# Where the group-norm variance of the previous head pair stands among the levels of the triangular inverse

## The chip, the cores and the metric

The kernel runs on one core of one Trainium2 chip. Its time is the device time of one execution in microseconds (us). Below, PE is TensorE, ACT is ScalarE, DVE is VectorE and POOL is GpSimd.

## The reference, cut to what matters

The reference is a network of three blocks on 1024 tokens of width 1024. The change touches one stage of the second layer, the RWKV-7 time mix, and there its scan over time with what follows it:

```python
def step(S, inp):
    r_t, w_t, k_t, v_t, a_t, b_t = inp
    sa = jnp.einsum('bhvk,bhk->bhv', S, a_t)
    S = S * w_t[:, :, None, :] + sa[..., None] * b_t[:, :, None, :] + v_t[..., None] * k_t[:, :, None, :]
    y = jnp.einsum('bhvk,bhk->bhv', S, r_t)
    return S, y
...
mean = jnp.mean(y, axis=-1, keepdims=True)
var = jnp.mean(jnp.square(y - mean), axis=-1, keepdims=True)
yn = ((y - mean) * lax.rsqrt(var + RW_GN_EPS)).reshape(B, T, D)
yn = yn * ln_w.astype(f32) + ln_b.astype(f32)
```

There are 16 heads of 64 channels. Also of this stage is the norm of each key, `kk / sqrt(sum(kk * kk))`.

## The kernel before, in words

The function `rw_core` computes the scan in chunks of 64 tokens. Two heads stand side by side on the 128 partitions, so the loop over `m` has eight head pairs, m = 0 to 7. For each pair a triangular matrix of each chunk is inverted, first in 2x2 blocks, then by doubling the block size. There are five levels, 0 to 4. At each of the levels 0 to 3, for each of the two heads h:

- TensorE multiplies (`corrections(m, lev, h)`, L2289, 32 matmuls of 64x32 in the profile's count),
- ScalarE copies the product out of PSUM in two instructions (`keep_correction`, L2507 and L2509),
- TensorE multiplies again (`inverses(m, lev, h)`, L2298, 32 matmuls),
- VectorE adds and transposes (`grow`, L2696 and L2698), and the next level's corrections of that head wait for it.

Level 4, the last, has smaller matmuls of 32x32 (`last_corrections`, L2305, and `last_inverses`, L2312). ScalarE copies with L2507 alone between them, and `whole` on VectorE (L2703) ends it. Then `solutions` (L2321), `bonus_sum` (L2215), `outputs` (L2330, L2345) and the next pair's first products follow on TensorE.

The pair before, m-1, is finished inside pair m. Its chunk states are stepped one after the other (L2223, L2225) while level 0 and level 1 run. ScalarE squares the deviations (`squares`, L2499), TensorE sums them over each head (`variance`, L2215 on `rw_end`, four matmuls of 128x512), ScalarE takes the logarithm (`log_variance`, L2491) and later exp(-0.5 x) of it (`inverse_deviation`, L2495), and VectorE scales with that (`group_norm`, L2663).

The pair after, m+1, is prepared inside pair m, too. The squares of its keys are summed by `key_sum` (L2215 on `rw_next`), and ScalarE takes their logarithm (`log_key`, L2483) and exponential (`inverse_key`, L2487). Then come an affine copy (`blend`, L2464) and another exponential (`decay_until`, L2468). Pair 0 has no pair before it, so no variance. Pair 7 has no pair after it, and ScalarE makes copies of rows for the next stage instead (`high`, L2477).

ScalarE holds the tables of one set of functions at a time. Where a logarithm follows an exponential or the other way round, an `ACT_TABLE_LOAD` stands ahead of the instruction.

The order of the work on each engine is the order in which the code is written; there is no scheduler. Engines wait for one another by semaphores, named in the code (`var_done`, `x_ready`, `dt_ready`). Where the variance stands among the levels on TensorE, in `rw_core`:

```python
inverses(m, 1, 1)
if prior:
    variance(m - 1)
for h in (0, 1):
    corrections(m, 2, h)
```

Of the kernel before, what the change touches and what calls it, by code (L numbers as in the profile page):

```python
# [2048 lines left out]
def rw_core(nc, g, block, nxt, small, mk, xh, xl):  # L2049
# [161 lines left out]
    def _(pe):  # L2211
# [16 lines left out]
        def variance(m):  # L2228
            pe.wait_ge(g.dev_ready.sem, g.dev_ready.base + m + 1)
            head_sum(dev, STEP_BANK, g.var_done)  # L2230
# [122 lines left out]
        for m in range(KD):  # L2353
            prior, following = m > 0, m + 1 < KD
            pe.wait_ge(g.hat_go.sem, g.hat_go.base + m + 1)
            if prior:
                pe.wait_ge(g.y1_ready.sem, g.y1_ready.base + m)
            if not prior:
                pe.wait_ge(g.acc_free.sem, first - 1)
            gram(X_BANK, at, bt, g.gram_n)  # L2360
            if not prior:
                pe.wait_ge(g.bonus_ready.sem, g.bonus_ready.base + 1)
                pe.wait_ge(g.acc_free.sem, first)
            pe.wait_ge(g.hat_ready.sem, g.hat_ready.base + m + 1)
            for j in range(NT):
                transposes(m, j)
                if prior and j:
                    step(m - 1, j if j < 4 else j + 1)
                if j == 3:
                    pe.wait_ge(g.prep_ready.sem, g.prep_ready.base + m + 1)  # L2370
                    pe.wait_ge(g.n_ready.sem, g.n_ready.base + m + 1)
                    gram(X_BANK, bt, rt, g.gram_rb)
                    if prior:
                        step(m - 1, 4)
            gram_ar(m)
            if prior:
                step(m - 1, 9)
            pe.wait_ge(g.rb_ready.sem, g.rb_ready.base + m + 1)
            for h in (0, 1):
                corrections(m, 0, h)  # L2380
                if prior:
                    step(m - 1, 10 + h)
            first_solution(m)
            for h in (0, 1):
                inverses(m, 0, h)
                if prior:
                    step(m - 1, 12 + h)
            for h in (0, 1):
                corrections(m, 1, h)
                if prior:  # L2390
                    step(m - 1, 14 + h)
            inverses(m, 1, 0)
            if following:
                pe.wait_ge(g.w_ready.sem, g.w_ready.base + 2 * m + 2)
                key_sum(m + 1)
            inverses(m, 1, 1)
            if prior:
                variance(m - 1)
            for h in (0, 1):
                corrections(m, 2, h)  # L2400
            for h in (0, 1):
                inverses(m, 2, h)
            for h in (0, 1):
                corrections(m, 3, h)
            for h in (0, 1):
                inverses(m, 3, h)
            for h in (0, 1):
                last_corrections(m, h)
            for h in (0, 1):
                last_inverses(m, h)  # L2410
            if prior:
                pe.wait_ge(g.y_ready.sem, g.y_ready.base + m)
            solutions(m)
            if following:
                bonus_sum(m + 1)
            outputs(m, prior, following)
# [27 lines left out]
    def _(act):  # L2444
# [44 lines left out]
        def log_variance(m):  # L2489
            act.wait_ge(g.var_done.sem, g.var_done.base + m + 1)  # L2490
            nc.scalar.activation(deviation_rates, deviation_rates, ACT.Ln, bias=norm_eps).then_inc(g.log_ready.sem, 1)  # L2491
# [20 lines left out]
        for m in range(KD):  # L2512
            prior, following = m > 0, m + 1 < KD
            act.wait_ge(g.gram_n.sem, g.gram_n.base + m + 1)
            nc.scalar.activation(both_of(Nlow), both(X_BANK)[:, :, 0:BLK], ACT.Copy)
            nc.scalar.activation(both_of(Nc), both(X_BANK)[:, :, BLK:CH], ACT.Copy, scale=lower).then_inc(g.n_ready.sem, 1)
            for j in range(NT):
                keep_tokens(m, j)
            keep_correction(m, 0, 0)
            keep_correction(m, 0, 1)  # L2520
            for h, hd in enumerate(heads):
                act.wait_ge(g.w1_done.sem, g.w1_done.base + 2 * m + h + 1)
                nc.scalar.activation(tok[:, :, W_, hd], bank(SUM_BANK + h), ACT.Copy).then_inc(g.w_ready.sem, 1)
            if following:
                key_copy(m + 1)
                decay(m + 1)
            keep_correction(m, 1, 0)
            if following:
                key_square(m + 1)
            else:  # L2530
                high(0)
            keep_correction(m, 1, 1)
            if following:
                growth(m + 1)
            else:
                high(1)
            if prior:
                squares(m - 1)
            if following:
                log_key(m + 1)  # L2540
            else:
                high(2)
            if prior:
                log_variance(m - 1)
            keep_correction(m, 2, 0)
            keep_correction(m, 2, 1)
            if following:
                inverse_key(m + 1)
            else:
                high(3)  # L2550
            keep_correction(m, 3, 0)
            keep_correction(m, 3, 1)
            if following:
                blend(m + 1)
            else:
                high(4)
            keep_correction(m, LAST, 0)
            if following:
                decay_until(m + 1)
            else:  # L2560
                high(5)
            keep_correction(m, LAST, 1)
            if prior:
                inverse_deviation(m - 1)
            for h, b in ((0, X_BANK), (1, D_BANK)):
                act.wait_ge(g.ug_done.sem, g.ug_done.base + 2 * m + h + 1)
                nc.scalar.activation(GU[:, h], g.ps[:, b:b + 2, :].rearrange("p b (j s) -> p (b j) s", j=4), ACT.Copy).then_inc(g.ug_ready.sem, 1)
            if not following:
                high(6)
            act.wait_ge(g.out_y.sem, g.out_y.base + m + 1)  # L2570
            nc.scalar.activation(paired_chunks(y1), pair(X_BANK), ACT.Copy).then_inc(g.y1_ready.sem, 1)
            if prior:
                act.wait_ge(g.normed.sem, g.normed.base + m)
            else:
                act.wait_ge(g.kept[1].sem, g.kept[1].base)
            act.wait_ge(g.out_z.sem, g.out_z.base + m + 1)
            nc.scalar.activation(paired_chunks(dev), pair(SUM_BANK), ACT.Copy).then_inc(g.z_ready.sem, 1)
# [1773 lines left out]
```

## Time and profile before

| What | Value |
| --- | --- |
| Median of 3 runs | 3553.84 us (3550.99 to 3561.1) |
| The profiled execution | 3547.82 us |
| Its span | 3546.0 us |
| TensorE busy | 3405.1 us, 96% of the span |
| ScalarE busy | 1194.9 us, 34% |
| VectorE busy | 1984.6 us, 56% |
| Mean granted TensorE clock | 0.982 of full speed |

The span is what the trace covers; 1.8 us lie around it. The eight pairs take the stretch from about 1590 to 2070 us of it, one pair some 57 us. Busy shares are means over all the stages, so a step of one pair is to be read from a timeline of that pair. The granted clock is 1.00 where TensorE runs at 2.4 GHz and 0.50 where it runs at 1.2 GHz.

### The profile page before, as it was taken

Reading aid. Unit: us, or ns where it says so; the run is one execution under the profiler, and the core shown is the slowest. Engines: PE = TensorE matmul, PEld = TensorE weight load, DVE = VectorE, ACT = ScalarE, POOL = GpSimd, SP = SyncE. Lnnn points to the kernel's source line nnn. Section 1 sums busy time; section 2 is a strip of 40 time slices with the busy share of each in tenths; the row PEclk is TensorE's granted clock in tenths of the full one; section 3 lists DMA queues with packets and bytes.
Section 4 is the critical chain, followed back from the end, with each engine's and each line's share of the span. In section 5 each row is a group of like instructions: output and inputs, shape, how many; then the busy total and the mean of one; then the engine's idle time right before and its main releaser. Section 6 shows DMA issues by size and latency. Waiting matters only on the chain. (4 is left out here: it accounts for less than half of the span.)

```text
span 3546.0 us, 61071 instructions
## 1 busy us (share of the span) xinstructions
PE 3405.1 (96%) x25028; PEld 2748.4 (78%) x25028; DVE 1984.6 (56%) x2398; ACT 1194.9 (34%) x1597; POOL 1590.5 (45%) x1148
## 2 busy tenths in 40 slices
PE   7998999999999999999999999999999999999989
PEld 5886778888888777888787877888888887674767
DVE  6886565556224652226767647555542458868452
ACT  4654233333102362226465524333310231242221
POOL 3442377775333323334344425877633323560352
PEclk9998999999999999999999999999999999999999
DMA  2111122224311142241212211222332113111212
GB/s 103 48 49 38 33 87 79 80 89 152 109 42 56 40 179 95 95 147 39 85 46 86 68 37 48 88 89 78 111 128 88 52 42 119 61 48 42 101 43 76
DMA packets 74063, 274.58 MB, mean 77 GB/s; under 512 B 8208, under 2 KB 8592, under 8 KB 73360
## 3 DMA queue, kind: packets, MB, share of 16 engines
q1 hardware_dynamic: 68112, 250.79, 20.8%
q10 hardware_dynamic: 5760, 20.97, 1.5%
q8 instruction: 153, 2.51, 0.3%
q14 instruction: 38, 0.31, 0.0%
HBM read 207.77 MB, written 63.96 MB: 77 GB/s over the span
## 5 line engine op out<-in xcount | busy, mean ns | idle before, releaser
L117 POOL TENSOR_TENSOR gap<-ones 128x1 f32<-128x1 f32 x150 | 46.0, 307 | 1238.8 <-PE ps L167 774.4
L120 POOL TENSOR_TENSOR wlo<-wraw,whi 128x1024 fp32r<-128x1024 f32 (+3 forms) x150 | 391.6, 2611 | 12.5
L893 DVE TENSOR_TENSOR h<-ps,h 128x1024 f32<-128x1024 f32 (+1 forms) x56 | 68.5, 1223 | 288.9 <-PE ps L416 259.6
L167 PE MATMUL ps<-xh,whi 128*128 128x512 f32 x640 | 203.0, 399 | 21.6 <-ACT rw_stage L1888 5.1
L167 PE MATMUL ps<-xl,whi 128*128 128x512 f32 x640 | 199.2, 393 | 0.0
L167 PE MATMUL ps<-xh,wlo 128*128 128x512 f32 x640 | 198.7, 392 | 0.0
L1007 POOL TENSOR_TENSOR wlo<-wraw,whi 128x512 fp32r<-128x512 f32 x126 | 166.3, 1335 | 52.6 <-ACT whi L1130 52.6
L118 POOL TENSOR_SCALAR whi<-wraw 128x1024 fp32r<-128x1024 f32 (+3 forms) x150 | 178.9, 1192 | 0.0
L384 ACT ACTIVATE sq<-h 128x1024 f32<-128x1024 f32 x32 | 34.0, 1061 | 394.1 <-DVE h L893 304.0
L2200 POOL TENSOR_TENSOR rw_levels<-rw_levels,rw_masks 128x512 f32<-128x512 f32 x64 | 87.2, 1378 | 177.2 <-PE ps L2289 140.8
L167 PEld LDWEIGHTS ps<-xh,whi 128*128 128x128 f32 x640 | 119.7, 190 | 56.6 <-issue 8.9
L1007 POOL TENSOR_TENSOR ffn_wl<-ffn_wsum,ffn_wh 128x512 fp32r<-128x512 f32 x84 | 111.6, 1328 | 110.7 <-ACT ffn_wh L1130 110.6
L167 PEld LDWEIGHTS ps<-xl,whi 128*128 128x128 f32 x640 | 121.3, 190 | 25.9
L167 PEld LDWEIGHTS ps<-xh,wlo 128*128 128x128 f32 x640 | 121.2, 189 | 25.8
L1288 DVE TENSOR_TENSOR sum_of_squares<-ffn_part,sq 128x512 f32<-128x512 f32 x84 | 132.6, 1578 | 9.3
L1130 ACT ACTIVATE whi<-wraw 128x512 fp32r<-128x512 f32 x126 | 79.2, 630 | 168.9 <-POOL wraw L1002 90.3
L1047 PE MATMUL ps<-xh_sums,whi 128*128 128x512 f32 x336 | 130.9, 390 | 2.2 <-ACT ffn_part L1143 2.2
L1047 PE MATMUL ps<-xh_sums,wlo 128*128 128x512 f32 x336 | 130.7, 389 | 0.0
L1047 PE MATMUL ps<-xl_sums,whi 128*128 128x512 f32 x336 | 130.7, 389 | 0.0
L433 DVE TENSOR_TENSOR sum_of_squares<-sum_of_squares,sq 128x1024 f32<-128x1024 f32 x48 | 93.7, 1951 | 56.9 <-ACT sq L384 38.7
L416 PE MATMUL ps<-xh_sums,whi 128*128 128x512 f32 x384 | 118.4, 390 | 0.4 <-POOL wlo L120 0.4
L416 PE MATMUL ps<-xh_sums,wlo 128*128 128x512 f32 x384 | 118.3, 389 | 0.0
(673 smaller groups left out, 9535.0 us busy)
## 6 DMA issues: line engine op xcount, KB each, us to landing
wraw<-w_ffn_in SPq DMA_DIRECT2D x88, 512.0 KB, 3.5
ffn_hidden<-sum_of_squares SPq DMA_DIRECT2D x44, 512.0 KB, 2.6
rw_next<-rw_kept SPq DMA_DIRECT2D x40, 512.0 KB, 5.1
wraw<-w_ffn_out SPq DMA_DIRECT2D x32, 512.0 KB, 3.6
ffn_stage<-ffn_hidden SPq DMA_DIRECT2D x30, 512.0 KB, 4.9
rw_kept<-rw_stage SPq DMA_DIRECT2D x24, 512.0 KB, 2.7
rw_kept<-rw_stage ACTq DMA_DIRECT2D x24, 512.0 KB, 2.7
wraw<-w_ple SPq DMA_DIRECT2D x16, 640.0 KB, 3.8
```

The costliest lines, as they stand in the source:

```text
L117: nc.gpsimd.tensor_tensor(g.gap[:, 0:1], g.ones[:, 0:1], g.ones[:, 0:1], ALU.mult)
L118: nc.gpsimd.tensor_scalar(g.whi[:, s, 0:w], g.wraw[:, s, 0:w], 1.0, 0.0, ALU.mult, ALU.add).then_inc(g.w_hi.sem, 1)
L120: nc.gpsimd.tensor_tensor(g.wlo[:, s, 0:w], g.wraw[:, s, 0:w], g.whi[:, s, 0:w].bitcast(F32), ALU.subtract).then_inc(g.w_split.sem, 1)
L167: last = nc.tensor.matmul(acc[:, hf, :], w[:, s, c:c + P], x[:, kt, hf * HALF:(hf + 1) * HALF], start=start and kt == 0 and n == 0, stop=s ...
L416: last = nc.tensor.matmul(acc[:, hf, :], w[:, s, c:c + P], x[:, hf, :], start=start and n == 0, stop=stop and n == 2)
L433: nc.vector.tensor_tensor(g.sumsq[:], g.sumsq[:], sq[:, s, :], ALU.add).then_inc(g.sq_used.sem, 1)
L893: nc.vector.tensor_tensor(ht, flat(banks(g, acc + 2 * s)), ht, ALU.add).then_inc(g.acc_free.sem, 1)
L1007: nc.gpsimd.tensor_tensor(packed(lo), raw[n], packed(hi).bitcast(F32), ALU.subtract).then_inc(g.weight_low.sem, 1)
L1047: last = nc.tensor.matmul(acc, w[:, k * P:(k + 1) * P], x[n][:, k, :], start=k == 0 and i == 0, stop=k == KD // 2 - 1 and i == 2)
L1130: nc.scalar.activation(packed(slot(n)[0]), raw[n], ACT.Copy).then_inc(g.weight_high.sem, 1)
L1288: nc.vector.tensor_tensor(hid[:, hf * HALF:(hf + 1) * HALF], (u3, up1)[hf], gated[hf], ALU.mult).then_inc(g.half_ready.sem, 1)
L2200: nc.gpsimd.tensor_tensor(halved(Nm[:, h]), twice(Nc[:, h]), mask_wide(f"off{b}"), ALU.mult).then_inc(g.off_ready.sem, 1)
```

## The change

On TensorE `variance(m - 1)` moves from behind `inverses(m, 1, 1)` to between the corrections and the inverses of level 3. On ScalarE `log_variance(m - 1)` moves from ahead of level 2's copies to behind level 3's. Nothing is added or taken out in the code.

```diff
             inverses(m, 1, 1)
-            if prior:
-                variance(m - 1)
             for h in (0, 1):
                 corrections(m, 2, h)
             for h in (0, 1):
                 inverses(m, 2, h)
             for h in (0, 1):
                 corrections(m, 3, h)
+            if prior:
+                variance(m - 1)
             for h in (0, 1):
                 inverses(m, 3, h)
...
                 log_key(m + 1)
             else:
                 high(2)
-            if prior:
-                log_variance(m - 1)
             keep_correction(m, 2, 0)
             keep_correction(m, 2, 1)
             if following:
...
             keep_correction(m, 3, 0)
             keep_correction(m, 3, 1)
+            if prior:
+                log_variance(m - 1)
             if following:
                 blend(m + 1)
             else:
```

How it moves the instructions of TensorE, in a middle pair; `rw_end` holds the squares of the deviations, `rw_next` those of the keys:

```order
 L2215 MATMUL ps<-rw_next_4823,rw_masks_4824 128x512 x2
 L2298 MATMUL ps<-rw_inverse_7338 64x32 x16
-L2215 MATMUL ps<-rw_end_7334,rw_masks_4824 128x512 x2
 L2289 MATMUL ps<-rw_inverse_7338,rw_levels_7337 64x32 x32
 L2298 MATMUL ps<-rw_inverse_7338 64x32 x32
 L2289 MATMUL ps<-rw_inverse_7338,rw_levels_7337 64x32 x32
+L2215 MATMUL ps<-rw_end_7334,rw_masks_4824 128x512 x2
 L2298 MATMUL ps<-rw_inverse_7338 64x32 x32
 L2305 MATMUL ps<-rw_inverse_7338,rw_levels_7337 32x32 x32
```

The two wide products (four in the profile's count) now stand three rows later. On ScalarE, ahead of the copies of level 2 of the same pair:

```order
 L2483 ACT_TABLE_LOAD
 L2483 ACTIVATE ps<-ps,wraw 128x1024
-L2491 ACTIVATE ps<-ps,wraw 128x1024
 L2507 ACTIVATE rw_inverse_7338<-ps,rw_masks_4824 128x8x32
 L2509 ACTIVATE rw_inverse_7338<-ps,rw_masks_4824 128x8x32
```

The second logarithm has left the first one's side. Behind the copies of level 3:

```order
 L2507 ACTIVATE rw_inverse_7338<-ps,rw_masks_4824 128x8x32
 L2509 ACTIVATE rw_inverse_7338<-ps,rw_masks_4824 128x8x32
+L2491 ACT_TABLE_LOAD
+L2491 ACTIVATE ps<-ps,wraw 128x1024
 L2464 ACTIVATE rw_next_4823<-rw_next_4823,rw_small_4822,vectors 128x1024
 L2507 ACTIVATE rw_inverse_7338<-ps,rw_masks_4824 128x8x32
+L2468 ACT_TABLE_LOAD
 L2468 ACTIVATE rw_next_4823<-rw_next_4823 128x1024
 L2507 ACTIVATE rw_inverse_7338<-ps,rw_masks_4824 128x8x32
```

It arrives there with a table load of its own, and the exponential L2468 gets one, too. That is so in the six pairs 1 to 6, so ScalarE has 1022 rows in place of 1010. In pair 7 its one load for L2491 moves along with it. The orders of VectorE, POOL and the DMA queue are unchanged.

## Rows read from the trace of the kernel before

**Rows 1.** Page, part 1: busy us, share of the span, instructions.

```profile
PE 3405.1 (96%) x25028; PEld 2748.4 (78%) x25028; DVE 1984.6 (56%) x2398; ACT 1194.9 (34%) x1597; POOL 1590.5 (45%) x1148
```

**Rows 2.** Timeline of TensorE, pair 3: start us, us, instruction, idle before it.

```profile
1783.00 1.12 PE L2298 MATMUL ps<-rw_inverse 64*64 64x32 f32 x32
1784.05 1.98 PE L2215 MATMUL ps<-rw_end,rw_masks 128*128 128x512 f32 x4
1785.96 2.05 PE L2289 MATMUL ps<-rw_inverse,rw_levels 64*64 64x32 f32 x64
1788.02 2.06 PE L2298 MATMUL ps<-rw_inverse 64*64 64x32 f32 x64
1790.24 2.05 PE L2289 MATMUL ps<-rw_inverse,rw_levels 64*64 64x32 f32 x64 [0.17 <-DVE rw_inverse L2698]
1792.29 2.06 PE L2298 MATMUL ps<-rw_inverse 64*64 64x32 f32 x64
1794.42 0.69 PE L2305 MATMUL ps<-rw_inverse,rw_levels 32*32 32x32 f32 x32
...
1797.00 1.06 PE L2312 MATMUL ps<-rw_inverse 32*32 32x32 f32 x32 [0.54 <-ACT rw_inverse L2507]
```

**Rows 3.** Timeline of ScalarE, pair 3.

```profile
1783.50 1.28 ACT L2483 ACT_TABLE_LOAD   x1
1784.79 1.09 ACT L2483 ACTIVATE ps<-ps,wraw 128x1024 f32<-128x1024 f32 x1
1786.07 1.09 ACT L2491 ACTIVATE ps<-ps,wraw 128x1024 f32<-128x1024 f32 x1 [0.19 <-PE ps L2215]
1787.13 0.47 ACT L2507 ACTIVATE rw_inverse<-ps,rw_masks 128x256 f32<-128x256 f32 x1
1787.50 0.47 ACT L2509 ACTIVATE rw_inverse<-ps,rw_masks 128x256 f32<-128x256 f32 x1
...
1792.34 0.47 ACT L2507 ACTIVATE rw_inverse<-ps,rw_masks 128x256 f32<-128x256 f32 x1
1792.71 0.47 ACT L2509 ACTIVATE rw_inverse<-ps,rw_masks 128x256 f32<-128x256 f32 x1
1793.07 1.24 ACT L2464 ACTIVATE rw_next<-rw_next,rw_small,vectors 128x1024 f32<-128x1024 f32 x1
1795.16 0.47 ACT L2507 ACTIVATE rw_inverse<-ps,rw_masks 128x256 f32<-128x256 f32 x1 [0.86 <-PE ps L2305]
1795.54 1.05 ACT L2468 ACTIVATE rw_next<-rw_next 128x1024 f32<-128x1024 f32 x1
1796.48 0.47 ACT L2507 ACTIVATE rw_inverse<-ps,rw_masks 128x256 f32<-128x256 f32 x1
```

**Rows 4.** Timeline of VectorE, pair 3.

```profile
1784.62 0.45 DVE L2698 STREAM_TRANSPOSE rw_inverse<-rw_inverse 128x256 f32<-128x256 f32 x1
```

**Rows 5.** Timelines of TensorE and ScalarE, pair 7.

```profile
2009.98 1.12 PE L2298 MATMUL ps<-rw_inverse 64*64 64x32 f32 x32 [0.40 <-ACT rw_inverse L2509]
2011.87 3.55 PE L2215 MATMUL ps<-rw_end,rw_masks 128*128 128x512 f32 x4 [0.77 <-ACT rw_end L2499]
...
2012.78 1.28 ACT L2491 ACT_TABLE_LOAD   x1
2015.46 1.09 ACT L2491 ACTIVATE ps<-ps,wraw 128x1024 f32<-128x1024 f32 x1 [1.39 <-PE ps L2215]
```

**Rows 6.** Stretches: us; busy (x) of PE, PEld, DVE, ACT, POOL; clock; DMA.

```profile
1613.90:1622.50 8.60, 8.43 (x264) 8.00 (x260) 4.70 (x9) 7.78 (x13) 4.40 (x3) 1.00 0.02 4
1786.00:1796.50 10.50, 9.98 (x353) 9.34 (x352) 5.91 (x10) 9.18 (x15) 6.41 (x5) 1.00 0.01 3
1796.70:1803.30 6.60, 6.30 (x82) 6.24 (x84) 5.65 (x8) 2.19 (x3) 1.22 (x1) 0.50 0.01 2
2011.70:2015.00 3.30, 3.13 (x4) 1.18 (x4) 0.36 (x1) 2.35 (x3) 0.00 (x0) 0.50 0.83 302
```

**Rows 7.** Timeline of TensorE, pair 0: the last inverses.

```profile
1625.16 0.69 PE L2312 MATMUL ps<-rw_inverse 32*32 32x32 f32 x32 [0.40 <-ACT rw_inverse L2507]
```

## The prediction

> **What bounds the kernel.** The page's first part comes first: TensorE is busy 96% of the span and no other engine above 56% [rows 1]. So a microsecond by which TensorE's last product of a pair moves is a microsecond of the kernel, unless a wait swallows it. Next come the timelines of one middle pair, pair 3. On TensorE [rows 2] the reader is to see that from 1783.00 to 1794.4 the levels run with one gap, 0.17 us: the engine is the path there. The first long wait, 0.54 us, is before the last inverses at 1797.00, and ScalarE's copy L2507 at 1796.48 ends it [rows 3]. Here ScalarE is the path: copy 1795.16, exponential L2468 at 1795.54, copy 1796.48. Last, the clock [rows 6]: full through the levels, 0.50 after them.
>
> **What is removed at level 2.** The variance holds TensorE from 1784.05 to 1785.96, 1.91 us, ahead of level 2's corrections. Without it, the first head's start at 1784.05, the second's when VectorE's transpose has ended, 1784.62 + 0.45 = 1785.07 [rows 4], plus 0.1 for the hand-over (with it the gap before 1790.24 is 0.17 [rows 2]): done about 1786.2. ScalarE is not free then. Its table load and the key's logarithm run until 1784.79 + 1.09 = 1785.88 as before. Without the second logarithm the copies start at 1785.85 instead of 1787.13, 1.28 us earlier. So the inverses of level 2 start at 1786.74 instead of 1788.02, and TensorE now waits some 0.5 us before them. **Gain: 1.28**, not 1.91.
>
> **What is added at level 3.** All of level 2 and level 3's corrections keep their pace, so the latter start at 1788.96 and end at 1791.01. Before, TensorE went on into the inverses without a gap, since the copy of one head hides behind the other head's corrections. There is no hole to put the variance into: all its 1.91 us count. The inverses start at 1792.92 instead of 1792.29. **Net so far +0.63.**
>
> **The two table loads.** The order shows them, 12 in all. The one for the logarithm does not wait for the variance: in pair 7 it ran at 2012.78 while its instruction waited until 2015.46 [rows 5]. In pair 3 the copies of level 3 then end at 1791.90, the load at 1793.20, the logarithm (1.09) at 1794.3, L2464 (1.24) at 1795.5. The copy behind it is due at 1795.16 + 0.63 = 1795.79. The first load fits, with 0.3 us to spare; cover gone, each further tenth would count. The second doesn't: copy at 1795.79 to 1796.26, load to 1797.55, exponential, copy of the second head at 1798.51 instead of 1796.48. **Last inverses, and the solutions behind them, +2.03 us** (0.63 and 1.40). That TensorE's 0.5 us wait becomes some 2 us. VectorE's and POOL's parts of the level are done by then, and everything after waits for TensorE, so nothing gives it back. No DMA is issued by the moved steps, and no queue is passed.
>
> A rule of the Trainium skill stands beside this, "ScalarE: Activation LUTs", What ACT_TABLE_LOAD costs: a switch costs 1.28 us and a drain of 1.38 on top. The row has the 1.28, and the instruction behind starts 0.01 us after it (1783.50, 1784.79) [rows 3]; the trace does not show the drain. Were it there, both loads would be on the path; that is the third rival.
>
> **Pair 7** has no key sum and no added load. Before, TensorE waited 0.40 and 0.77 us there and the four variance matmuls took 3.55 us instead of 1.98, at clock 0.50 [rows 5, 6]. At full clock the new order lets the inverses of level 2 start about 2013.6 (behind `high`) and not 2017.4, and adds 1.91 later: -1.9. Should the clock fall there as it did, the variance still costs 3.5, and five blocks of level matmuls are slower by 0.75 each (below): -3.8 + 3.5 + 3.7 = +3.4. I take +1.
>
> **The clock, where I had to choose.** Until now a dense piece (128 rows by 512 columns) stood every few microseconds among the small matmuls. After the change only 64x32 matmuls run from 1783.0 to 1791.0, 8 us, with waits of 0.1, 0.5 and 0.17 us. What does the trace say of such a stretch? Pair 0 is the upper side: no variance, small matmuls from 1613.9 to 1622.5, waits 0.17 us each, clock 1.00 [rows 6]. Pair 7 is the lower side: small matmuls and 1.17 us of waits, and the clock was 0.50 at once. And in every pair the still smaller matmuls of level 4, with gaps, lose it: full until 1796.5, then 0.50 to 1803.3 although TensorE was busy 6.30 of 6.60 us [rows 6]. Once lost, it came back only after dense products. My 0.77 us of waits lie between 0.34 and 1.17. I take the lower side, since a step from 64x32 to 32x32 without any long gap was enough at level 4: the levels seem to hold the clock with little to spare. The Trainium skill, "TensorE: Matmul & The Clock Gate", Part 1, says that the slow clock is the default and that only activity lifts it; it speaks against the change for that reason, and the rows agree.
>
> Price of a fall about 1788: a half level of inverses and both blocks of corrections, 2.5 blocks. A block of 32x32 matmuls took 0.69 us at 1.00 [rows 7] and 1.06 at 0.50 [rows 2]: +0.37. A block of 64x32 takes 1.03; at most it doubles. No row has one at 1.2 GHz, so 0.37 to 1.03, and I take 0.75 (an estimate; the ratio of the two rows without the last matmul's 0.2 us is 1.8): 1.9 us. The variance, then at half clock, +1.57 (3.55 against 1.98). Together **+3.5**, from 2.5 to 4.1; the waits for ScalarE are no longer than before and hide none of it.
>
> **The sum:** six pairs at 2.03 + 3.5 = 5.5 give 33, pair 7 gives 1: **+34 us**. The profiled execution took 3547.82, which makes 3581.8. It lies 6 us below the median of the runs shown, and I forecast the median: 3553.84 + 34 = **3588**.
>
> **Rivals.**
>
> 1. *The clock holds* in the levels, as in pair 0. For it: 0.77 us of waits in 8 is little. Then 6 x 2.03 - 1.9 = +10.3: 3564. Chance 0.20. That is on the edge of what a measurement of this kernel tells from no change, 0.3% or 10.7 us.
> 2. *Faster.* If at level 3 TensorE has to wait for ScalarE's copy anyway, the variance fills that wait. It decides from a wait of 1.91 us before the inverses; with the loads hidden in the slack of later copies, the gain of 1.28 in six pairs and 3.8 in pair 7 would stay whole: -11.5, 3542. Against it: the row at 1792.29 shows no wait, and ScalarE reaches that copy with 0.3 us in hand after its own load. Chance 0.04.
> 3. *A load holds ScalarE for longer than its row*, say for its 1.28 us once more, so that the first one is on the path as well: the second adds 1.28, the first 1.28 - 0.3. That is 2.3 in six pairs on rival 1's sum: +24, 3578. Against it: the instruction behind a load starts at once [rows 3]. Chance 0.04. With the skill page's drain of 1.38 it would be +25, 3579.
> 4. *The change doesn't do what it says*: the order shows that it does.
>
> The forecast has 0.72. Its own range: 2.03 + 2.5 to 2.03 + 4.1 in six pairs and -1.9 to +3.4 in pair 7 is +25 to +40, and where the low clock ends inside the solutions shifts from pair to pair by up to 1 us, which gives 3574 to 3600. For 8 in 10 the range must take in part of rival 1: 3561 to 3601. Slower by over 0.3%: 0.72 + 0.04 + a third of rival 1, 0.83. Within 0.3%: 0.13. Faster: 0.04.
>
> **What would show it.** Table loads: 12 more, each 1.28. Level 2's inverses 3.7 us after the level 1 inverses of the second head, not 5.0. The wait for ScalarE's L2507 before the last inverses grows from 0.54 to about 2 us. Granted clock 0.50 somewhere in the second half of the levels in pairs 1 to 6, with variance matmuls that take over 3 us for four; if the clock is 1.00 there, that step is wrong and rival 1 is right. A wait before level 3's inverses ended by ScalarE would mean that its slack was misread.

## The result and the profile after

| | before | changed |
| --- | --- | --- |
| Median | 3550.99 us (3550.01 to 3561.1, 5 runs) | 3582.97 us (3571.93 to 3593.31, 5 runs) |
| Profiled execution, its span | 3547.82, 3546.0 | 3571.93, 3570.1 |
| Granted clock, mean | 0.982 | 0.977 |

The ratio is 1.009, 95% interval 1.0076 to 1.0104: **32 us slower**. In a second measurement of the unchanged new kernel (the first experiment below) the ratio was again 1.009.

The page's first part for the changed kernel answers to [rows 1]:

```profile
PE 3421.8 (96%) x25028; PEld 2759.1 (77%) x25028; DVE 1985.7 (56%) x2398; ACT 1209.4 (34%) x1609; POOL 1590.8 (45%) x1148
```

TensorE does the same 25028 instructions and is 16.7 us longer busy. So part of the loss is the same work at a lower clock. ScalarE has 12 instructions and 14.5 us more. The groups by line say which they are (durations are min/median/max in ns; before, L2491 had one load and L2468 none):

```profile
L2491 ACT ACT_TABLE_LOAD  x7: 1283/1283/1283, 1677.7 to 2039.8; - x7
L2468 ACT ACT_TABLE_LOAD  x6: 1283/1283/1283, 1683.8 to 1984.7; - x6
```

Timeline of TensorE in pair 2 of the changed kernel, to be laid beside [rows 2]:

```profile
1728.61 1.12 PE L2298 MATMUL ps<-rw_inverse 64*64 64x32 f32 x32
1729.56 1.10 PE L2289 MATMUL ps<-rw_inverse,rw_levels 64*64 64x32 f32 x32
1730.83 1.12 PE L2289 MATMUL ps<-rw_inverse,rw_levels 64*64 64x32 f32 x32 [0.17 <-DVE rw_inverse L2698]
1732.30 2.06 PE L2298 MATMUL ps<-rw_inverse 64*64 64x32 f32 x64 [0.34 <-ACT rw_inverse L2509]
1734.52 3.21 PE L2289 MATMUL ps<-rw_inverse,rw_levels 64*64 64x32 f32 x64 [0.16 <-DVE rw_inverse L2698]
1737.65 3.78 PE L2215 MATMUL ps<-rw_end,rw_masks 128*128 128x512 f32 x4
1741.36 2.28 PE L2298 MATMUL ps<-rw_inverse 64*64 64x32 f32 x64
1743.71 0.69 PE L2305 MATMUL ps<-rw_inverse,rw_levels 32*32 32x32 f32 x32
...
1747.71 1.06 PE L2312 MATMUL ps<-rw_inverse 32*32 32x32 f32 x32 [1.72 <-ACT rw_inverse L2507]
```

Three things are to be seen. The inverses of level 2 start at 1732.30, 3.69 us after the level 1 inverses of the second head (1728.61), where before it was 5.02. The corrections of level 3 take 3.21 us instead of 2.05 and the variance behind them 3.78 instead of 1.98, although the only wait from there to the inverses of level 3 is 0.16 us: the clock fell. The stretch view of 1734.5 to 1741.4 has it at 0.54 (last columns: clock, DMA share, GB/s):

```profile
1734.50:1741.40 6.90, 6.88 (x70) 4.30 (x70) 1.99 (x3) 3.75 (x6) 0.66 (x1) 0.54 0.01 2
```

And the wait before the last inverses is 1.72 us instead of 0.54. ScalarE in the same pair, beside [rows 3]:

```profile
1738.62 1.28 ACT L2491 ACT_TABLE_LOAD   x1
1741.47 1.09 ACT L2491 ACTIVATE ps<-ps,wraw 128x1024 f32<-128x1024 f32 x1 [1.57 <-PE ps L2215]
1742.48 1.23 ACT L2464 ACTIVATE rw_next<-rw_next,rw_small,vectors 128x1024 f32<-128x1024 f32 x1
1744.45 0.47 ACT L2507 ACTIVATE rw_inverse<-ps,rw_masks 128x256 f32<-128x256 f32 x1 [0.74 <-PE ps L2305]
1744.95 1.28 ACT L2468 ACT_TABLE_LOAD   x1
1746.24 1.06 ACT L2468 ACTIVATE rw_next<-rw_next 128x1024 f32<-128x1024 f32 x1
1747.20 0.46 ACT L2507 ACTIVATE rw_inverse<-ps,rw_masks 128x256 f32<-128x256 f32 x1
```

The first load ran while TensorE was still at the variance, and cost nothing. The second stands between the two copies of level 4, and TensorE waits for the second copy.

In pairs 3 and 6 of this execution the clock did not fall. Pair 3, TensorE:

```profile
1788.57 0.31 PE L2298 MATMUL ps<-rw_inverse 64*64 64x32 f32 x4 [0.35 <-issue]
1788.81 1.98 PE L2215 MATMUL ps<-rw_next,rw_masks 128*128 128x512 f32 x4
...
1793.87 2.25 PE L2298 MATMUL ps<-rw_inverse 64*64 64x32 f32 x64
1796.09 2.25 PE L2289 MATMUL ps<-rw_inverse,rw_levels 64*64 64x32 f32 x64
1798.26 1.99 PE L2215 MATMUL ps<-rw_end,rw_masks 128*128 128x512 f32 x4
1800.18 2.06 PE L2298 MATMUL ps<-rw_inverse 64*64 64x32 f32 x64
...
1806.30 0.80 PE L2312 MATMUL ps<-rw_inverse 32*32 32x32 f32 x32 [1.96 <-ACT rw_inverse L2507]
```

Here TensorE lost 0.35 us of its own accord ahead of the key sum. It reached level 2's inverses when ScalarE's copy was done, so the wait of 0.34 is missing, and everything up to level 4 ran at full clock. This is the same program a pair later. In pair 6 the wait before level 2's inverses was there, but 0.21 us long and not 0.34.

In a table, per pair: us from the level 1 inverses of the second head to the inverses of level 2, from there to those of level 3, from there to the solutions.

| | before | changed, clock fell | changed, clock held |
| --- | --- | --- | --- |
| middle pairs | 5.03, 4.27, 5.4 to 5.7 | 3.69, 9.06 to 9.32, 7.1 to 7.3 (pairs 1, 2, 4, 5) | 3.15, 6.31, 6.85 (pair 3); 3.55, 6.12, 7.05 (pair 6) |
| their sum | 14.7 to 15.0 | 20.1 | 16.3 and 16.7 |
| pair 7 | 7.43, 4.27, 5.70 | 3.95, 10.52, 5.70 | |

### The profile page after: what moved, and what is told of

Same layout as the page of the kernel before. It is cut to its first block and busy times, and to the rows that moved or that the text cites. A ratio compares the mean times of both kernels' runs of the same rounds, so it can differ in the third digit from the quotient of the medians.

```text
span 3570.1 us, 61083 instructions
## 1 busy us (share of the span) xinstructions
PE 3421.8 (96%) x25028; PEld 2759.1 (77%) x25028; DVE 1985.7 (56%) x2398; ACT 1209.4 (34%) x1609; POOL 1590.8 (45%) x1148
## 5 line engine op out<-in xcount | busy, mean ns | idle before, releaser
L1047 PE MATMUL ps<-xl_sums,whi 128*128 128x512 f32 x336 | 130.9, 390 | 0.0
L1047 PE MATMUL ps<-xh_sums,wlo 128*128 128x512 f32 x336 | 130.9, 390 | 0.0
L416 PE MATMUL ps<-xl_sums,whi 128*128 128x512 f32 x384 | 118.3, 390 | 0.0
```

Of the source, the lines that this page charges most:

```text
L416: last = nc.tensor.matmul(acc[:, hf, :], w[:, s, c:c + P], x[:, hf, :], start=start and n == 0, stop=stop and n == 2)
L1047: last = nc.tensor.matmul(acc, w[:, k * P:(k + 1) * P], x[n][:, k, :], start=k == 0 and i == 0, stop=k == KD // 2 - 1 and i == 2)
```

## The experiments

The diffs are against the changed kernel, except where "before" stands. The kernel before was measured beside them each time: its median was 3551.57 beside experiments 2, 3, 4 and 9, 3550.61 beside 1, 5, 7 and 8, 3550.86 beside 6 and 10, 3548.79 beside 11 and 3551.13 beside 12. `keep_busy` issues dense products of 128x512 on TensorE into a bank of PSUM that is free just then; nobody reads them, and in the profile they are L156. The waits that stand ahead of them in the diffs are for the last reader of that bank.

**1. The changed kernel once more** (no edit).

> The changed kernel once more, beside the others of this call. Theory: 3583 us again, and the low clock in the levels follows the wait before level 2's inverses pair by pair: where TensorE comes late to level 2 by a pause of its own, that wait is 0.17 us instead of 0.34 and the clock holds (two of six pairs in the first profile); where it is 0.34 the level 2 and 3 stretch takes 9 us and not 6.3.

Measured: 3584.14 (3579.81 to 3587.03, 6 runs), ratio 1.009 [1.0074, 1.0106]. In its profile, with a span of 3582.9 near the median, the clock fell in all of pairs 1 to 7. The wait before level 2's inverses was 0.35 us in five of the six middle pairs and 0.28 in the sixth, so the low clock went with the wait, as expected; there was no pair without it. TensorE in its pair 3:

```profile
1798.24 2.69 PE L2298 MATMUL ps<-rw_inverse 64*64 64x32 f32 x64 [0.35 <-ACT rw_inverse L2509]
1800.74 3.61 PE L2289 MATMUL ps<-rw_inverse,rw_levels 64*64 64x32 f32 x64
1804.28 3.78 PE L2215 MATMUL ps<-rw_end,rw_masks 128*128 128x512 f32 x4
1807.99 3.63 PE L2298 MATMUL ps<-rw_inverse 64*64 64x32 f32 x64
```

These are the rows that were missing: 64 matmuls of 64x32 at 1.2 GHz take 3.61 us, against 2.05. Summed over pairs 1 to 6, the stretch from the level 1 inverses of the second head to the solutions takes 124.9 us against 89.6 before, +35.3; the solutions behind them are 2.5 us shorter in sum. From pair 0's solutions to the last chunk step it is 466.6 against 431.4 us, and that is nearly all of the span's +36.9.

**2. Hold the clock, leave the rest**: two dense products where the 0.34 us wait was.

```diff
             for h in (0, 1):
                 corrections(m, 2, h)
+            if prior:
+                pe.wait_ge(g.dev_ready.sem, g.dev_ready.base + m)
+                keep_busy(nc, g, STEP_BANK, 2)
             for h in (0, 1):
                 inverses(m, 2, h)
```

> The changed kernel, with two dense products (128x128 by 512 columns, their result is not used) on TensorE behind level 2's corrections in pairs 1 to 7, where TensorE waited 0.34 us for ScalarE. Theory (the clock): the wait is filled, TensorE stays at 2.4 GHz through the levels of pairs 1 to 6, level 3's corrections take 2.05 us and the variance 1.98 in all of them, and what is left is the table loads and the 0.6 us of the variance: 3561 to 3566 us, some 18 us below the changed kernel. Rival (not the clock, but a wait or a contention that the variance meets at its new place): the two products only add their time, the levels stay as slow, 3583 to 3586.

Measured: 3569.78 (3564.17 to 3576.6, 6 runs), ratio 1.0045 [1.0031, 1.0059]. Its pair 2, TensorE:

```profile
1733.69 0.61 PE L156 MATMUL ps<-ident 128*128 128x512 bf16 x2
1734.23 2.06 PE L2298 MATMUL ps<-rw_inverse 64*64 64x32 f32 x64
1736.45 2.05 PE L2289 MATMUL ps<-rw_inverse,rw_levels 64*64 64x32 f32 x64 [0.17 <-DVE rw_inverse L2701]
1738.44 1.98 PE L2215 MATMUL ps<-rw_end,rw_masks 128*128 128x512 f32 x4
```

All six middle pairs read 3.81, 6.12, 7.0 to 7.1: 17.05 in all but one, in place of 20.1, and 2.05 more than before. The 0.6 us of useless work take 3 us off a pair and 13 us off the kernel. That is the clock's part, and 2.05 a pair is the chain's. It stayed 4 us above what was expected of it. In the profiled run, which is 7 us above the median, the tail behind pair 7's solutions took 39.5 us in place of 29.8 (last section).

**3. Without the two added table switches** (the logarithm of the variance is left out; an affine copy of the same size stands in its place).

```diff
-            nc.scalar.activation(deviation_rates, deviation_rates, ACT.Ln, bias=norm_eps).then_inc(g.log_ready.sem, 1)
+            nc.scalar.activation(deviation_rates, deviation_rates, ACT.Identity, bias=norm_eps).then_inc(g.log_ready.sem, 1)
```

> The changed kernel, with an affine copy in place of the logarithm in the variance's rate (the logarithm is left out of the computation), so that pairs 1 to 6 have no second and third table switch. Theory: the load behind the first copy of level 4 was on the path with 1.3 to 1.4 us, the one behind level 3 hidden or nearly so; the wait before the last inverses goes from 1.7 to 2.0 us back to about 0.5 and the time falls by 8 to 10 us, to 3573 to 3575. The clock falls in the same pairs as before, since its cause (the wait at level 2) is not touched. Rival (loads cost nothing, all of the loss is the clock's): within 2 us of the changed kernel. Rival (each load costs double its row): 3560 or below.

Measured: 3577.37 (3572.13 to 3582.07, 6 runs), ratio 1.0066 [1.0051, 1.0081]. That is 5.6 to 6.8 us less than the changed kernel, not 8 to 10. The last part of a pair is 5.3 to 6.1 in five of six pairs, so the wait is gone, but the clock fell in every pair, and in pair 3 it stayed low for 20.5 us (granted 0.50 from 1796.5 to 1817.0). More was lost behind the levels: in five pairs the rows of the solutions took 5.9 to 6.2 us, in the changed kernel 5.0 to 5.5 in all, since more of the low clock fell on them.

**4. Before, with ScalarE's half of the change alone.**

```diff
-            if prior:
-                log_variance(m - 1)
             keep_correction(m, 2, 0)
             keep_correction(m, 2, 1)
...
             keep_correction(m, 3, 1)
+            if prior:
+                log_variance(m - 1)
```

> The kernel before, with the logarithm of the variance moved on ScalarE alone, to behind level 3's copies; TensorE's order is the one before. Theory: TensorE loses nothing and gains nothing up to level 3 (the level 2 inverses stay 5.0 us behind the level 1 inverses of the second head, since the variance holds TensorE), the clock stays at 2.4 GHz through the levels, and both loads and the logarithm now stand before the copies of level 4 with no 1.28 us won earlier: 1.6 us from the first and 1.4 from the second, 3.0 in six pairs and 1.3 in pair 7, so +19 us, 3570. Rival (loads are hidden): within 3 us of the kernel before.

Measured: 3569.28 (3563.82 to 3572.24, 5 runs), ratio 1.0048 [1.0034, 1.0063]: +17.7. All six middle pairs read 5.03, 4.27, 8.58; the last part is 2.9 longer. TensorE from level 4 on, in pair 3:

```profile
1797.51 0.69 PE L2305 MATMUL ps<-rw_inverse,rw_levels 32*32 32x32 f32 x32
...
1800.23 1.06 PE L2312 MATMUL ps<-rw_inverse 32*32 32x32 f32 x32 [1.01 <-ACT rw_inverse L2507]
1802.96 1.07 PE L2312 MATMUL ps<-rw_inverse 32*32 32x32 f32 x32 [1.67 <-ACT rw_inverse L2507]
```

Without the variance to hide it, the first load reaches the path as well. From L2305 to the last inverses it is 5.45 us, against 2.58 before, and 2.87 is two loads and 0.3. The 0.3 belong to the logarithm, which moved, too: its 1.09 us used up the 0.86 that ScalarE had idle there before [rows 3]. The clock held in levels 2 and 3, with the variance at its old place. So the 17.7 us come without any fall of the clock there. They are no share of the 32, since in the changed kernel the variance hides the first load.

**5. The square later**: the changed kernel, with ScalarE's `squares(m - 1)` moved from ahead of the key's logarithm to behind level 2's copies. It takes the 0.34 us wait away by having the copies ready, without any added work.

```diff
-            if prior:
-                squares(m - 1)
             if following:
                 log_key(m + 1)
...
             keep_correction(m, 2, 1)
+            if prior:
+                squares(m - 1)
```

> The changed kernel, with ScalarE's squares of the deviations moved from ahead of the key's logarithm to behind level 2's copies (the variance at its new place needs them only there). No dummy work. Theory: ScalarE reaches level 2's first copy 1.05 us earlier, the wait before level 2's inverses shrinks to 0.17 us as in pair 0, and the clock holds at 2.4 GHz in the levels of all pairs: 3.15 us from the level 1 inverses of the second head to level 2's, 6.2 from there to level 3's, 7.1 on to the solutions, 16.4 against 15.0 of the kernel before and 19 to 20 of the changed one; time 3559 to 3563. Rival (the small matmuls lose the clock even without that wait, as the levels now hold no dense product for 8 us): as slow as the changed kernel less 3 us, 3580.

Measured: 3563.03 (3556.99 to 3566.9, 12 runs), ratio 1.0032 [1.0021, 1.0043]. Twenty us of the 32 are gone. Some 2.5 of them come from shorter levels at the same clock: a pair takes 16.65 us here and 17.05 in experiment 2. All six middle pairs read 3.14, 6.31, 7.0 to 7.2; the stretch view of pair 2's level 2 and 3 has the clock at 1.00, pair 7 has it at 0.56, and its levels took 21.8 us against 17.4 before:

```profile
1730.10:1738.50 8.40, 8.37 (x203) 6.74 (x199) 3.83 (x7) 8.10 (x12) 3.40 (x3) 1.00 0.01 2
2019.10:2041.00 21.90, 21.54 (x422) 18.46 (x422) 7.61 (x15) 13.32 (x19) 7.85 (x6) 0.56 0.40 134
```

**6. The same without the two added switches** (again the logarithm is left out).

> The changed kernel with the squares behind level 2's copies (so that the clock holds) and with an affine copy in place of the logarithm in the variance's rate (the logarithm is left out of the computation), so that pairs 1 to 6 have no second and third table switch. Theory: the 7.2 us from level 3's inverses to the solutions become 5.4 to 5.8, 1.4 to 1.8 us less in six pairs and nothing in pair 7: 9 to 10 us below the kernel with the late squares, 3553 to 3555, which leaves only the 1.91 us of the variance, less what its absence gives at level 2. Rival (a load is hidden or free): within 2 us of 3563. Rival (each load costs double its row): 3545 or below.

Measured: 3557.02 (3538.34 to 3560.46, 12 runs), ratio 1.0008 [0.9992, 1.0023]. The pairs read 3.15, 6.31, 5.70: 1.5 less each, as in the chain, and 0.15 from the kernel before. With the clock held and the loads gone, nothing measurable is left of the change; the interval allows from 3 us less to 8 us more. The gain against experiment 5 is 6.0, where 9 to 10 had been expected. The levels of the six pairs did take 8.9 us less, but their solutions took 2.1 more, and in this profile the tail took 38.2 us.

**7. Two loads a pair, at another place**: experiment 5, with both logarithms behind level 3's copies and the three exponentials behind level 4's (VectorE's `unit_key` moves behind `whole`, too).

```diff
-            if following:
-                log_key(m + 1)
-            else:
+            if not following:
                 high(2)
             keep_correction(m, 2, 0)
...
-            if following:
-                inverse_key(m + 1)
-            else:
+            if not following:
                 high(3)
             keep_correction(m, 3, 0)
             keep_correction(m, 3, 1)
+            if following:
+                log_key(m + 1)
             if prior:
                 log_variance(m - 1)
...
             keep_correction(m, LAST, 0)
+            if not following:
+                high(5)
+            keep_correction(m, LAST, 1)
+            if following:
+                inverse_key(m + 1)
+            if prior:
+                inverse_deviation(m - 1)
             if following:
                 decay_until(m + 1)
-            else:
-                high(5)
-            keep_correction(m, LAST, 1)
-            if prior:
-                inverse_deviation(m - 1)
```

> The changed kernel rebuilt on ScalarE so that the tables are switched twice in a pair and not four times: squares behind level 2's copies, both logarithms behind level 3's, both exponentials and the key's behind level 4's copies; on VectorE the key's scaling moves behind the last level. Theory: nothing of ScalarE but copies stands in the levels, the wait before the last inverses falls below 0.5 us, from level 1's last inverses to the solutions 3.15 + 6.2 + 5.0 = 14.4 us against 15.0 before, VectorE's chain starts 1.5 us later relative to the solutions but has 2.4 us in hand: 3546 to 3549. Rival (VectorE's chain becomes the path and costs 1 to 1.5 us a pair): 3556 to 3560. In both cases the clock in levels 2 and 3 stays at 2.4 GHz.

Measured: 3561.31 (3552.69 to 3567.94, 12 runs), ratio 1.0029 [1.0018, 1.0041]; no better than experiment 5. ScalarE in pair 3:

```profile
1792.14 1.28 ACT L2483 ACT_TABLE_LOAD   x1
1793.44 1.09 ACT L2483 ACTIVATE ps<-ps,wraw 128x1024 f32<-128x1024 f32 x1
1794.45 1.08 ACT L2491 ACTIVATE ps<-ps,wraw 128x1024 f32<-128x1024 f32 x1
1795.44 1.24 ACT L2464 ACTIVATE rw_next<-rw_next,rw_small,vectors 128x1024 f32<-128x1024 f32 x1
1796.58 0.83 ACT L2507 ACTIVATE rw_inverse<-ps,rw_masks 128x256 f32<-128x256 f32 x2
```

One load and three wide instructions now stand ahead of level 4's first copy. Corrections ended near 1795.9, the copy came at 1796.58. VectorE is late behind them, too. Its L2613 (`key_rate`) waits for L2464 and stands ahead of `whole` (L2703), and TensorE's solutions wait for `whole`; the profile puts that wait down to "issue":

```profile
1796.71 2.10 DVE L2613 TENSOR_TENSOR rw_next<-rw_next 128x1024 f32<-128x1024 f32 x1 [0.62 <-ACT rw_next L2464]
1798.74 0.86 DVE L2703 SCALAR_TENSOR_TENSOR rw_inverse<-ps,rw_masks,rw_inverse 128x256 f32<-128x256 f32 x2
```

```profile
1799.31 6.29 PE L2321 MATMUL ps<-rw_tok,rw_inverse 64*64 64x128 f32 x64 [0.75 <-issue]
```

So the last part takes 6.23 us where 5.0 had been forecast, and five of the six middle pairs read 3.14, 6.31, 6.23. That is 1.0 us a pair less than in experiment 5, and yet not clearly seen in the time. Pair 4 reads 3.14, 8.21, 5.56. Nothing but 0.17 us was waited for in its levels 2 and 3, and the clock fell in the variance all the same (3.68 us), against what was expected:

```profile
1846.56 2.45 PE L2289 MATMUL ps<-rw_inverse,rw_levels 64*64 64x32 f32 x64
1848.94 3.68 PE L2215 MATMUL ps<-rw_end,rw_masks 128*128 128x512 f32 x4
```

**8. The dense products at level 2 and among level 4.**

```diff
+            if prior:
+                pe.wait_ge(g.dev_ready.sem, g.dev_ready.base + m)
+                keep_busy(nc, g, STEP_BANK, 2)
...
+            keep_busy(nc, g, SUM_BANK, 1)
             last_corrections(m, 1)
+            keep_busy(nc, g, SUM_BANK, 1)
             last_inverses(m, 0)
+            keep_busy(nc, g, SUM_BANK, 6)
             last_inverses(m, 1)
```

> The changed kernel with two dense products (result not used) in the wait before level 2's inverses and eight among level 4's small matmuls, where TensorE now waits 2 us for ScalarE behind the table load. Theory: the clock holds from level 2 into the solutions, which then take 3.4 us instead of 5.0 in all pairs, at no cost as the wait is longer than the products: 1.5 us in eight pairs less than with the two products alone, 3558. Rival (VectorE's chain becomes the path): 3565. Rival (clock falls all the same): 3572.

Measured: 3562.6 (3544.38 to 3572.81, 12 runs), ratio 1.0023 [1.0006, 1.004]. All middle pairs 3.81, 6.12, 6.75, and the row of the solutions is 3.71 us long in place of the 5.0 to 6.4 of the kernel before (3.44 to the start of the last matmul, as the expectations count it). Pair 7 fell to a low clock behind a pause of 1.64 us at level 1 (it reads 6.22, 10.55, 6.66), and its tail took 38.6 us.

**9 and 10. Before, with dense products among level 4** (1, 1 and 2 of them), in all pairs, and in all but pair 7. The diff is the second half of experiment 8's, with 2 in place of 6.

> The kernel before, with four dense products (result not used) on TensorE among the small matmuls of level 4 in all pairs, where TensorE waits 0.24 and 0.54 us. If small matmuls with gaps are what loses the clock there, it now stays at 2.4 GHz into the solutions, which take 3.5 us and not 4.8 to 6.1; the products themselves cost 0.1 to 0.3 us a pair: 12 to 16 us less than before, 3535 to 3539. Rival A: the clock is held, but VectorE's chain of the next pair's preparation, which had 2.4 us in hand, becomes the path and takes half of it back: 3543. Rival B: the clock falls all the same, and the products cost 2 us in all: 3553.

> The kernel before, with four dense products (result not used) among level 4's small matmuls in pairs 0 to 6 but not in pair 7, where they cost 2.3 us in the first try. Theory: the solutions run at 2.4 GHz and take 3.44 us in seven pairs, each pair is 1.5 us shorter than before and pair 7 as before, 3541. Rival (what the clock gives back there is lost again in stages behind, as the timed median of the first try was only 1.4 us below the kernel before): 3547 to 3550.

Measured: 3550.17 (3541.98 to 3558.78, 12 runs), ratio 0.9992 [0.998, 1.0005], and 3549.98 (3540.45 to 3558.72, 12 runs), ratio 0.9996 [0.9984, 1.0009]. Neither reached its forecast; 3547 to 3550 is what experiment 10's rival had said. The profiles show the gain in the middle: a pair takes some 55.5 us instead of 57.3, since the clock is full through the solutions. They also show where it goes. With the products in pair 7 its last part is 7.96 instead of 5.70 and the tail 34.4 instead of 29.8; without them pair 7 reads 9.04, 6.83, 7.47 and the tail 39.9.

**11 and 12. The same, with pair 7 held as well**, by products at its level 1; and that with one more product behind each step of the tail.

```diff
             inverses(m, 1, 0)
+            pe.wait_ge(g.w_ready.sem, g.w_ready.base + 2 * m + 2)
             if following:
-                pe.wait_ge(g.w_ready.sem, g.w_ready.base + 2 * m + 2)
                 key_sum(m + 1)
+            else:
+                keep_busy(nc, g, SUM_BANK, 4)
             inverses(m, 1, 1)
+            if not following:
+                keep_busy(nc, g, SUM_BANK, 3)
...
             piece(0, 2 * cc - 1)
+            keep_busy(nc, g, 7, 1)
```

The last added line is in experiment 12 alone.

> The kernel before, with four dense products (result not used) among level 4's small matmuls in all eight pairs, and in pair 7, which has no key sum, four more before level 1's last inverses and three before the variance, where TensorE waited 0.40 and 0.77 us and the clock fell. Theory: in the first two tries pairs 1 to 6 were 1.5 to 2 us shorter each, and pair 7, where the clock fell and stayed low for 8 and 22 us, gave it back; with the clock held there as well the stretch of the eight pairs is 12 to 15 us shorter than before and the time 3537 to 3540. Rival (the timed runs lose it in later stages whatever the pairs do): 3548 to 3551 with the shorter stretch of pairs all the same.

> The kernel with the clock held in all eight pairs, with one more dense product (result not used) in each of the 15 steps of the last pair's states that run between pieces of the output projection. In the traces so far this tail took 29.1 to 30.1 us from the solutions of pair 7 where those began at 1.2 GHz, and 34 to 40 us, at 1.2 GHz nearly throughout, where they ran at 2.4 from the start. Theory: the tail sits at the edge of the clock, one more dense product a step keeps it at 2.4 GHz and costs at most 0.2 us a step: 30 to 33 us instead of 38.4, the stretch from the first solutions to the last step 417 to 420 us (431.4 before), time 3536 to 3541. Rival (the product only adds its time and the clock falls all the same): 3548 to 3551.

Measured: 3545.56 (3535.04 to 3555.93, 11 runs), ratio 0.9988 [0.9977, 0.9999], and 3545.79 (3537.79 to 3550.9, 12 runs), ratio 0.9986 [0.9977, 0.9994]. Both are a little faster than either kernel: 3 and 5 us below the kernel before, 37 below the changed one. Two stretches of the kernel before and of experiment 11, from pair 0's solutions to pair 6's, and the tail (columns as in [rows 6]):

```profile
1625.80:1969.80 344.00, 319.47 (x8692) 275.81 (x8688) 242.39 (x448) 192.34 (x282) 138.55 (x90) 0.95 0.19 64
2027.40:2057.20 29.80, 26.89 (x531) 20.20 (x528) 18.48 (x40) 7.87 (x9) 3.19 (x1) 0.92 0.01 3
```

```profile
1630.10:1961.10 331.00, 311.42 (x8720) 262.43 (x8714) 239.83 (x448) 192.12 (x282) 143.39 (x89) 1.00 0.20 67
2016.70:2055.10 38.40, 33.97 (x531) 22.98 (x528) 18.49 (x40) 6.69 (x8) 3.20 (x1) 0.70 0.01 2
```

The middle gains 13 us at clock 1.00, and the tail gives 8.6 back at 0.70. Over the whole stretch to the last step that profile is 6.5 us shorter than the one before. Outside of it, in unchanged code, it took 10.6 us longer, so a part of such a gain drowns in the scatter of the other stages. The product behind each step (experiment 12) made the tail 35.0 us at clock 0.90, no better in the median. The stretch came to 429.0 us, not 417 to 420, and in its pair 4 the clock fell at level 4 in spite of the products. Both medians lie above their forecasts.

## Why the prediction was right

It forecast +34 us, 3588, in a range of 3561 to 3601, and named two causes; the median came out 32 us higher, at 3582.97. By its own steps:

- **Level 2.** Inverses 3.74 us after the level 1 inverses, not 5.02: it was 3.69. The wait in front of them was put at 0.5 and measured 0.34. Right.
- **Variance at level 3 costs its whole 1.91.** No wait stood before level 3's inverses in any profile, and with the clock held (experiment 2) level 2's inverses to level 3's took 6.12 against 4.27, +1.85. Right, and it is what rival 2 needed to be otherwise.
- **Two loads, one hidden.** Forecast: 0.3 us to spare for the first, +1.40 for the second. Where the clock held (pair 3) the copy that came next waited 0.28 us for its matmuls. From L2305 to the last inverses it was 4.00 us in pair 2 and 3.99 in pair 3 against 2.58 before, so +1.42. Experiment 4 took the cover off the first load, and then both counted. The forecast chain of 2.03 a pair stands beside 2.05 in experiment 2.
- **The clock falls.** This was the step where the prediction chose, and it came true in 4 of 6 middle pairs of the first profile and 6 of 6 of the second. That the low clock was a cause and no companion is shown by experiments 2 and 5, which both kept it at 1.00 in the middle pairs, one with added work and one without any, and gave back 13 and 20 us. The reason it gave was half right. It counted on 8 us without a dense piece together with 0.77 us of waits. The waits were 0.67 (0.17, 0.34, 0.16), and they mattered: experiment 5 has 7.5 us of nothing but small matmuls with 0.17 us of waits, and held the clock in six of six pairs.
- **Two of its readings were wrong.** Pair 0 had one wait of 0.17 us in its 8.6 us (8.60 - 8.43 [rows 6]), so its side of the comparison is 0.17 and not 0.34; the choice stays the same. And the clock did not come back only after dense products. In pair 4 of the kernel before it was at 0.98 from 1858 to 1859 and at 1.00 from then on, inside the solutions' 64x128 matmuls, with the next 128x512 product at 1860.04.
- **Its price.** A block of 64x32 matmuls was estimated 0.75 slower; it is (3.61 - 2.05) / 2 = 0.78. The variance was put at +1.57 and cost +1.80. How long the low stretch lasts varies: the fall came in level 3's corrections in pair 2, which ends as +3.1 us (20.1 against 15.0 + 2.03), and already in level 2's inverses in pair 3 of experiment 1, where it lasted into the solutions (+5.3 by the same count). By experiment 1 the six pairs are at +35.3, or 5.9 each, against 5.5 forecast: 3.9 for the clock in place of 3.5, inside its 2.5 to 4.1. The solutions gave 2.5 of it back, which the forecast had only as scatter. So the sum came out closer than its terms: by that profile the clock and pair 7 cost some 3.5 us more than forecast, and the shorter solutions hid most of it. That part is luck.
- **Pair 7** was put at +1 (from -1.9 to +3.4). It took 20.2 us instead of 17.4, +2.8 (with a pause of 0.78 us in it that the change doesn't explain), and +2.3 in experiment 1: the clock fell, and the upper end was the better guess.

**The rivals.** *The clock holds* is refuted for the kernel as a whole, and true of two pairs of the first profile: its +10.3 stands beside the +11.7 us of experiment 2 from pair 0's solutions to pair 7's, and beside the +12.4 of experiment 5's median. *Faster* fell with the missing wait. *A load holds ScalarE for longer* fell too: in pair 3 of the changed kernel the load at 1799.23 is followed by its instruction at 1800.52, 1.29 us later, in experiment 4 both loads with what the logarithm adds cost 2.87, and leaving them out at a held clock gained 1.5 a pair. The Trainium skill ("ScalarE: Activation LUTs", What ACT_TABLE_LOAD costs) adds a drain of 1.38 us to each switch; these runs show none, and the measurement decides.

The prediction also leaned on the Trainium skill's "TensorE: Matmul & The Clock Gate", Part 1, by which the slow clock is the default. The runs bear on it only in part: TensorE was busy 6.88 of 6.90 us in pair 2 at a granted 0.54, so the busy time of the profile alone does not tell whether the clock is up.

What stays open is what tips the clock. The wait before level 2's inverses is one cause. In the profiles of the changed kernel and of experiments 1 and 3, the clock fell in each of the 16 middle pairs with a wait of 0.28 to 0.35 us. It held in the one with 0.21 and in the one with none. In the kernels without that wait (experiments 2, 5, 6, 7 and 8) it held in 29 of 30. The wait is not the only cause: the thirtieth is pair 4 of experiment 7, and pair 7 of experiment 5 fell in level 2's corrections, with 0.17 us of waits there and 0.40 before. No run varied the wait's length step by step.

## What to carry to other kernels

A wide product among small ones does two jobs: its own, and covering the time that TensorE would else wait for another engine. Here the uncovered 0.34 us cost the clock. Before moving such a product, look at which wait it covers, and price the small matmuls and the moved product itself at the lower clock, too. On ScalarE, count the switches between logarithm and exponential that a new order makes, and then ask of each load which copy stands behind it: the first here was free and the second cost its full length. And test a suspected clock loss with a small product at the suspected spot, since 0.6 us of it separated the two causes here, or take the wait away by an order, as experiment 5 did without any added work.

## What the runs showed that had not been expected

**A third of a microsecond decided 3 us.** In the same program, pair 3 of the first profile kept its clock after an unrelated pause 5 us earlier had let ScalarE's copy get ahead. That reading rests on one pair, but experiment 5 bears it out: with ScalarE's copies ready in time, six of six middle pairs held it. In experiment 7, with copies as early, five of six did.

**The tail behind pair 7 has two paces.** It is one chain of chunk steps with a pair of wide products between them. The kernel before ran it in 29.8 us, experiment 11 in 38.4. One step of each, TensorE:

```profile
2045.59 0.33 PE L2223 MATMUL ps<-wraw,rw_end 64*64 64x64 f32 x4
...
2045.97 0.73 PE L2423 MATMUL ps<-rw_o_xh,whi 128*128 128x512 f32 x2
2046.63 0.33 PE L2223 MATMUL ps<-wraw,rw_end 64*64 64x64 f32 x4
```

```profile
2046.04 0.48 PE L2223 MATMUL ps<-wraw,rw_end 64*64 64x64 f32 x4
...
2046.67 1.22 PE L2434 MATMUL ps<-rw_o_xh,whi 128*128 128x512 f32 x2
2047.82 0.48 PE L2223 MATMUL ps<-wraw,rw_end 64*64 64x64 f32 x4
```

(L2434 is L2423, shifted by the added lines.) A step takes 1.04 us in the first and 1.78 in the second, with the engine busy throughout in both. In seven profiles the tail took 29.1 to 30.1 us, and in all of them part of pair 7's solutions had run at the low clock (their row is 5.4 to 6.3 us long). In the four profiles in which that row is 3.71 us long, at full clock, it took 38.2 to 39.5. The remaining three (experiments 9, 10 and 12) lie at 34.4, 39.9 and 35.0 with rows of 4.9 to 6.2. So there is no clean rule, and experiment 12's expectation stated one too firmly: in experiment 10 the solutions began at the low clock, and the tail was the slowest of all. There is one profile of each kernel, and the cause wasn't tested. The 8 to 10 us are more than the shortfalls of experiments 2, 6 and 8 against their forecasts. They may be why the runs of experiment 8 lie 28 us apart, while those of the kernel before lie within 11 to 24: in experiment 8 the mean granted clock goes with the time, from 0.989 in the fastest run (3544.38) to 0.982 in the slowest (3572.81). Where in those runs the clock was lost isn't recorded.
